# A retention and short-convolution step on one core: normalised y turned through DRAM and VectorE's block transposes, and both prompt-state products behind chunk 23

## The reference

```python
scores = jnp.einsum('bhld,bhmd->bhlm', q, k) * dmask
out = (jnp.einsum('bhlm,bhmv->bhlv', scores, v)
       + jnp.einsum('bhld,bhdv->bhlv', q, S) * q_decay[:, :, None])
S_new = S * s_decay[:, None, None] + jnp.einsum('bhmd,bhmv->bhdv', k * k_decay[:, :, None], v)
...
mu = jnp.mean(yf, axis=-1, keepdims=True)
var = jnp.mean(jnp.square(yf - mu), axis=-1, keepdims=True)
yn = ((yf - mu) * lax.rsqrt(var + GN_EPS)).astype(h.dtype)
yn = yn.transpose(0, 2, 1, 3).reshape(B, L, RET_V)
return (jax.nn.silu(g) * yn) @ w_out, S_new
```

## Time and profile before

| what | value |
|---|---|
| median of 3 runs | 1662.14 us (1662.13 to 1662.34) |
| the profiled execution | 1662.3 us |
| its span, first to last instruction | 1660.7 us |
| granted TensorE clock, mean | 0.997 |
| PE busy | 1641.7 us (99%) |
| DVE busy | 1048.8 us (63%) |
| ACT busy | 594.8 us (36%) |
| POOL busy | 163.3 us (10%) |
| data moved by DMA | 338.47 MB, 204 GB/s |

### The profile page before, as it was taken

One profiled execution on the slowest core, in us unless ns is written; L12 is line 12 of the kernel. 1 busy time (PEld: TensorE's weight loads), 2 busy tenths in 40 slices (PEclk: granted clock), 3 DMA queues, 4 the chain that ended last, 5 costly groups with the idle time before them and its releaser, 6 DMA issues.

```text
span 1660.7 us, 30156 instructions
## 1 busy us (share of the span) xinstructions
PE 1641.7 (99%) x10864; PEld 1582.0 (95%) x10864; DVE 1048.8 (63%) x1671; ACT 594.8 (36%) x814; POOL 163.3 (10%) x241
## 2 busy tenths in 40 slices
PE   9999999999999999999999999999999999999996
PEld 9999989989999999999998998999999999999995
DVE  6566556556656656656655655977766666666465
ACT  4333333333333333333233333543333334343333
POOL 1001101101100100100100110510000000000243
PEclk9999999999999999999999999999999999999998
DMA  8647947946855864884794793445744444444442
GB/s 324 215 143 259 321 139 256 316 139 224 318 192 171 310 229 156 279 294 142 264 323 135 256 325 116 156 136 182 257 153 146 152 144 144 147 151 143 146 146 101
DMA packets 125208, 338.47 MB, mean 204 GB/s; under 512 B 27248, under 2 KB 43248, under 8 KB 125120
## 3 DMA queue, kind: packets, MB, share of 16 engines
q1 hardware_dynamic: 104768, 263.10, 47.4%
q0 software_dynamic: 20352, 74.08, 12.5%
HBM read 280.08 MB, written 46.28 MB: 197 GB/s over the span
## 4 chain that ended last, share of the span: by engine, by line
PE 97%; ACT 1%; DVE 1%; DMA 0%; issue 0%; POOL 0%; SPq 0%; ACTq 0%; DVEq 0%; POOLq 0%
PE proj L1313 25%; PE proj L1318 25%; PE proj L1314 25%; PE proj L1450 5%; PE proj L1458 4%; PE proj L1451 4%; PE qs L1409 2%; PE side L1297 1%; PE side L1299 1%; PE side L1298 1%; PE side L1341 1%; PE side L1304 1%; ACT residual L692 0%; PE proj L1476 0%; PE qs L1414 0%; PE side L1380 0%
## 5 line engine op out<-in xcount | busy, mean ns | idle before, releaser
L1313 PE MATMUL proj<-x_hi,w_hi 128*128 128x322 f32 (+2 forms) x2512 | 763.0, 314 | 0.0
L1314 PE MATMUL proj<-x_lo,w_hi 128*128 128x322 f32 (+2 forms) x2512 | 759.1, 312 | 0.0
L571 ACT CAST w_hi<-w_raw 128x1024 fp32r<-128x1024 f32 x416 | 436.1, 1049 | 588.3 <-PE proj L1314 386.9
L812 DVE TENSOR_TENSOR w_lo<-w_raw,w_hi 128x1024 fp32r<-128x1024 f32 x416 | 512.2, 1234 | 146.2 <-ACT w_hi L571 91.9
L1313 PEld LDWEIGHTS proj<-x_hi,w_hi 128*128 128x128 f32 x2512 | 473.8, 189 | 5.4 <-issue 4.4
L1314 PEld LDWEIGHTS proj<-x_lo,w_hi 128*128 128x128 f32 x2512 | 473.0, 188 | 0.4
L1318 PE MATMUL proj<-x_hi,w_lo 128*128 128x322 f32 (+2 forms) x2512 | 428.5, 313 | 0.3 <-DVE w_lo L812 0.3
L1318 PEld LDWEIGHTS proj<-x_hi,w_lo 128*128 128x128 f32 x2512 | 389.2, 189 | 0.5 <-DVE w_lo L812 0.5
L1450 PE MATMUL proj<-qk_or_z,w_hi 128*128 128x322 f32 x480 | 147.0, 316 | 0.6 <-DVE qk_or_z L1022 0.2
L1451 PE MATMUL proj<-qk_or_z,w_hi 128*128 128x322 f32 x480 | 144.0, 310 | 0.0
L844 DVE SCALAR_TENSOR_TENSOR state_update<-state_update,state_decay_of_head,side 128x512 f32<-128x512 f32 x128 | 94.0, 734 | 17.5 <-PE side L1341 14.5
(11 more groups left out here) (211 smaller groups left out, 1276.8 us busy)
## 6 DMA issues: line engine op xcount, KB each, us to landing
w_raw<-w_head SPq DMA_DIRECT2D x256, 512.0 KB, 4.4
w_raw<-w_conv SPq DMA_DIRECT2D x128, 512.0 KB, 3.5
state_update<-s_in POOLq DMA_DIRECT2D x64, 512.0 KB, 7.2
s_out<-state_update POOLq DMA_DIRECT2D x64, 512.0 KB, 5.6
te_for_q_or_prompt_state<-s_in SPq DMA_DIRECT2D x32, 512.0 KB, 7.6
w_raw<-w_cout SPq DMA_DIRECT2D x32, 512.0 KB, 3.5
v_scratch<-v_turned_or_y_norm SPq DMA_DIRECT2D x32, 176.0 KB, 5.4
v_rows<-v_scratch SPq DMA_DIRECT2D x8, 512.0 KB, 4.7
```

Source lines behind the costliest of these rows:

```text
L571: act.copy(w_hi[:, i % SPL, :], w_raw[:, i % RAW, :]).then_inc(w_h.sem, 1)
L812: TT(w_lo[:, i % SPL, :], w_raw[:, i % RAW, :], f(w_hi[:, i % SPL, :]), ALU.subtract).then_inc(w_l.sem, 1)
L1313: mm(bank[:, 0:n], wh[:, k, :], rhs_h(k), start=(first and k == 0), stop=False)
L1314: x = mm(bank[:, 0:n], wh[:, k, :], rhs_l(k), start=False, stop=False)
```

## The change

y's tiles are computed with full 128 rows, so that row r of tile t is token 128 t + r: 14 columns of zeros are put ahead of the first tile's scores (`A_AT`). TensorE makes the tiles in the order 0, 2, 1. VectorE takes all three statistics and the variance in side 19 and normalises in side 20, in that order too. SyncE stores each normalised tile (128 x 512, 256 KB) to a DRAM scratch ahead of its load of chunk 25, and ahead of its load of chunk 26 waits for the three stores and reads them back in four parts, so that 32 partitions hold one 32-token row of each of 12 blocks. In side 23 VectorE waits for the four reads and turns the 32 x 32 blocks in four instructions into PSUM, from where the gating reads as before. To fit the blocks, the columns of the gate's weights and the rows of the out weights are permuted on the host. The twelve transposes on TensorE are gone. Both groups of prompt-state products stand behind chunk 23, both of ScalarE's copies of them in side 24, ahead of them the fourth z part; and the stack copies of v that stood behind the loads of chunks 24 and 25 stand behind that of chunk 23.

```diff
-A_AT = [0, NP_ + NSAMP, NP_ + NSAMP + SC[1][1] + NSAMP]
+A_AT = [CUT, CUT + NP_, CUT + NP_ + SC[1][1]]
...
-VS_AT = {22: (8, 9, 10, 11), 23: (0, 1, 2), 24: (3, 4, 5), 25: (6, 7)}
+VS_AT = {22: (8, 9, 10, 11), 23: (0, 1, 2, 3, 4, 5, 6, 7)}
+Y_OUT, Y_BACK = 25, 26
...
+        y_b = vt_yn[:, :].rearrange("p (t n) -> p t n", t=YB)
+        y_dram = nc.dram_tensor("y_scratch", [YB, 32, DV], F32).ap()
+        yt_bank = [bank_r[2], bank_r[0], bank_r[1], bank_q]
...
+                    if i == Y_OUT:
+                        for n, t in enumerate((0, 2, 1)):
+                            sp.wait_ge(y_nm.sem, y_nm.at(h, n + 1))
+                            sp.dma_start(y_dram[4 * t:4 * t + 4, :, :].rearrange("a p n -> (a p) n"),
+                                         y_n[:, t, :]).then_inc(yd_out.sem, 16)
+                    if i == Y_BACK:
+                        sp.wait_ge(yd_out.sem, yd_out.at(h, yd_out.per))
+                        for a in range(4):
+                            sp.dma_start(y_b[32 * a:32 * a + 32, :, :],
+                                         y_dram[:, :, P * a:P * a + P].rearrange("t p e -> p t e")).then_inc(yd_in.sem, 16)
                     load_chunk(0, h, CPH, i, w_head[h, i])
...
-                        act.wait_ge(y_done.sem, y_done.at(h, 3))
+                        act.wait_ge(y_done.sem, y_done.at(h, 2))
                         act.copy(y_n[0:META, 2, :], bank_q[32:32 + META, :]).then_inc(yp_out.sem, 1)
                     if i == 24:
                         z_round(3)
-                    if i in (23, 24):
-
-                        d = i - 23
+                    for d in range(DKB) if i == 24 else ():
                         act.wait_ge(st_done.sem, st_done.at(h, d + 1))
...
+                    def turned(j):
+
+                        dve.transpose(yt_bank[j][:, 0:3 * P].rearrange("p (t e) -> p t e", e=32),
+                                      y_b[:, :, 32 * j:32 * j + 32]).then_inc(yt_done.sem, 1)
...
+                    if i == 23:
+                        dve.wait_ge(yd_in.sem, yd_in.at(h, yd_in.per))
+                        turned(0)
+                        turned(1)
+                        gated(0)
+                        turned(2)
+                        gated(1)
+                        z_rest(0)
+                        turned(3)
+                        gated(2)
+                        z_rest(1)
+                        z_rest(2)
+                    if i == 24:
+                        gated(3)
+                        z_rest(3)
...
-                    if i == 23:
-                        y_turn(3)
-                    if i in (22, 23):
-
-                        d = i - 22
+                    for d in range(DKB) if i == 23 else ():
                         if not d:
...
-                    if i == 22:
-                        y_turn(0, 1, 2)
...
-    w_v = w_in[:, 2 * qk:2 * qk + dv].reshape(D, HEADS, 4, DVB, 32).transpose(0, 1, 3, 2, 4).reshape(D, dv)
-    b = blocks(np.concatenate([w_in[:, 0:2 * qk], w_v, w_in[:, 2 * qk + dv:]], 1), 8)
+    w_vg = w_in[:, 2 * qk:].reshape(D, 2 * HEADS, 4, DVB, 32).transpose(0, 1, 3, 2, 4).reshape(D, 2 * dv)
+    b = blocks(np.concatenate([w_in[:, 0:2 * qk], w_vg], 1), 8)
...
-    wo = A(w_ret_out)[0].reshape(HEADS, DVB, P, KT // 2, 2 * P).transpose(0, 3, 2, 1, 4)
+    wo = A(w_ret_out)[0].reshape(HEADS, 4, DVB, 32, KT // 2, 2 * P).transpose(0, 4, 1, 3, 2, 5)
```

More of the change, by code:

```diff
@@ L54 @@
 A_LEN = A_AT[2] + SW
-Y_ROWS = [QRY[0][1], QRY[1][1], SW]
+YB = 3 * P // 32
 Y_TAIL = QRY[2][0] + 2 * META
@@ L244, in hybrid_step @@
         v_dram = nc.dram_tensor("v_scratch", [TB, 32, DV], F32).ap()
+        y_dram = nc.dram_tensor("y_scratch", [YB, 32, DV], F32).ap()
+        yd_out, yd_in = count("y_rows_out", 3 * 16), count("y_blocks_in", 4 * 16)
         tab_in = count("tab_in")
@@ L987, in side @@
                         dve.tensor_copy(sd_h[:, :], sdec[:, bass.ds(h, 1)]).then_inc(sd_set.sem, 1)
[L988 to L991, removed]
+                    if i == 19:
+                        for n, t in enumerate((0, 2, 1)):
+                            dve.wait_ge(y_done.sem, y_done.at(h, n + 1))
                             if t == 2:
@@ L996, in side @@
                                 dve.wait_ge(yp_add.sem, yp_add.at(h))
-                            dve.bn_stats(stat[0:rows, t, :], y_bank[t][0:rows, :]).then_inc(y_st.sem, 1)
-                            dve.wait_ge(y_st.sem, y_st.at(h, t + 1))
+                            dve.bn_stats(stat[:, t, :], y_bank[t][:, :]).then_inc(y_st.sem, 1)
+                            dve.wait_ge(y_st.sem, y_st.at(h, n + 1))
                             dve.sem_inc(passed.sem, 1)
-                            dve.bn_aggr(mv[0:rows, t, :], stat[0:rows, t, :]).then_inc(y_ag.sem, 1)
@@ L1001, in side @@
-                    if i == 20:
+                            dve.bn_aggr(mv[:, t, :], stat[:, t, :]).then_inc(y_ag.sem, 1)
                         dve.wait_ge(y_ag.sem, y_ag.at(h, 3))
                         dve.tensor_scalar(gvar[:, :], mv[:, :, 1], GN_EPS, None, add).then_inc(y_ve.sem, 1)
-                    if i == 21:
+                    if i == 20:
                         dve.wait_ge(y_rs.sem, y_rs.at(h))
[L1006 to L1022, removed]
+                        for t in (0, 2, 1):
+                            dve.tensor_scalar(y_n[:, t, :], y_bank[t][:, :], mv[:, t, 0:1], rstd[:, t:t + 1],
+                                              ALU.subtract, ALU.mult).then_inc(y_nm.sem, 1)
@@ new lines, in turned, with gated @@
+                    def turned(j):
+                        dve.transpose(yt_bank[j][:, 0:3 * P].rearrange("p (t e) -> p t e", e=32),
+                                      y_b[:, :, 32 * j:32 * j + 32]).then_inc(yt_done.sem, 1)
+                    def gated(j):
+                        dve.wait_ge(yt_done.sem, yt_done.at(h, j + 1))
+                        dve.wait_ge(p_act.sem, p_act.at(h, 1 + j))
+                        if j >= 2:
+                            dve.wait_ge(z_l.sem, z_l.at(h, j - 1))
+                        c0, c1 = CUT, CUT + Y_TAIL
+                        TT(tmp[:, j % 2, 0:Y_TAIL], yt_bank[j][:, c0:c1], gate[:, j, 0:Y_TAIL], ALU.mult)
+                        groups = yt_bank[j][:, c1:c1 + 96].rearrange("p (c i) -> p c i", i=32)[:, :, META:]
+                        rest = lambda ap: ap.rearrange("p (c i) -> p c i", i=META)
+                        TT(rest(tmp[:, j % 2, Y_TAIL:N]), groups, rest(gate[:, j, Y_TAIL:N]), ALU.mult).then_inc(z_f.sem, 1)
@@ new lines, in z_rest @@
+                    def z_rest(j):
+                        dve.wait_ge(z_h.sem, z_h.at(h, j + 1))
+                        TT(z_lo[:, j, :], tmp[:, j % 2, 0:N], f(z_hi[:, j, :]), ALU.subtract).then_inc(z_l.sem, 1)
+                    if i == 23:
[10 more added lines that the diff above has]
+                        z_rest(2)
@@ L1299, in three @@
                 return mm(out, a_lo_, b_hi_, start=False, stop=stop)
-            def turn(out, src):
-                n = src.shape[0]
-                return pe.transpose(out, src if src.dtype == F32 else src.bitcast(F32), ident[0:n, 0:n])
             def proj(base, r, per, i, bank, n, rhs_h, rhs_l, first, last, by_block=None):
@@ L1349, in head @@
             def head(h, first, last=False):
[L1350 to L1360, removed]
                 def side(i):
@@ L1418, in side @@
                         pe.wait_ge(a_l.sem, a_l.at(h, 3))
[L1419 to L1423, removed]
+                        at, kr = A_AT[2], KEY[2][1]
+                        for t in (0, 2, 1):
+                            if t == 2:
+                                x = three(bank_q[:, :], a_hi[0:kr, at:at + SW], a_lo[0:kr, at:at + SW], v_hi[0:kr, 2, :],
+                                          v_lo[0:kr, 2, :], False, True)
+                            for m in range(t + 1) if t < 2 else ():
+                                own = A_AT[m] + P * t - CUT - SC[m][0]
+                                x = three(bank_r[t][:, :], a_hi[:, own:own + P], a_lo[:, own:own + P],
                                           v_hi[:, m, :], v_lo[:, m, :], m == 0, m == t)
                             x.then_inc(y_done.sem, 1)
[L1426 to L1429, removed]
                     for back, t in due(KV_AT, i, first, last):
                         kv_multiply(h, t, back)
-                    if i == 22:
-                        y_turn(0, 1, 2)
                 def out(i):
```

## The result

The changed kernel takes 1685.7 us in the median (1683.4 to 1688.7, 4 runs); the kernel before, beside it, 1662.2. The ratio is 1.0141 (95% interval 1.0129 to 1.0153). Forecast were 1653.4 us and a range of 1649 to 1660, so the time moved 23 us the wrong way, and lies above the late case (1671) too.

What follows compares the result with a forecast made beforehand. TensorE was taken to bound the kernel. Per head, -1.28 (transposes) -0.31 (old wait) +0.5 (new wait) = -1.09 us; eight heads -8.7, so 1662.1 - 8.7 = 1653.4 us, range 1649 to 1660.

Steps and rivals of the forecast that it cites:

- the late case: Rival 2: the trip through DRAM takes v's prices, TensorE waits 2.7 us a head, 1671 us; chance 0.11.
- TensorE's part: In each head twelve transposes go, 1.28 us; y products and moved prompt-state products cost the same as before.
- the old wait: Before, the out product's weight load on TensorE waited for VectorE's z low part: 0.31 us a head, forecast to go.
- The price of the trip: y's stores and reads through DRAM on SyncE's queue: from the last store issued at 357.7 to landing at 366.5.
- The end of normalising: VectorE's third normalisation of y ends at 357.65, with GpSimd's power taking 0.88 us beside VectorE's low part.
- The stores: SyncE's three stores of normalised y tiles: the last issued at 357.7, landed 3.6 us later.
- The reads: SyncE's four reads of 192 KB: 1.6 us to the fourth issue, then 3.6 us to landing.
- My upper end: Bound on the trip from v's own trip under full DMA load, 4.7 us taken twice: reads landed at 368.7.
- S: Time at which the reads have landed and VectorE's first block transpose starts; forecast 366.5.
- From landing to z the chain: Block transposes, gating and z parts on VectorE and ScalarE: z part 3's low part ends at S + 7.6.
- The price of a wait: TensorE's new wait near chunk 24: near 0.5 us a head, with the clock taken as unchanged.
- Rival 2: The data is late: S = 368.7, wait 2.7 us a head against 1.59 saved, 1671 us; chance 0.11.

Runs made afterwards that it cites:

- the same idea in a better order: Changed kernel with chunk 20 ahead of statistics, reads ahead of chunk 25's load, chunk 24's cast before z high parts, fourth gate between second and third: 1652.5 us.

## Why the prediction was wrong, step by step

**TensorE's part was right.** Twelve transposes 1.18 us a head (1.28 forecast), the old wait 0.31, the moved state products nothing (the wait is all that their run gained). The wider y tile cost nothing that could be told: its products start 0.23 us apart, as before.

**The price of the trip was wrong, by 3.1 us a head.** In its steps, as means over the heads, from TensorE's arrival:

- The end of normalising: -14.4, forecast 357.65 - 372.83 = -15.2. 0.8 us late, all of it the power, which I took at the 0.88 of the earlier trace rows and called hidden beside VectorE. There the power had started ahead of VectorE's low part; here it starts just behind it, and takes 1.0 us more.
- The stores: 4.0 us to the reads' issue, forecast 3.65. Right to 0.4. The head's table, which the prediction named beside the stores and did not price, has a share by the trace: in head 7, which loads none, it was 2.9. In head 6 it was 6.0, and there GpSimd issued the table 1.3 us later than in the other heads, so that its packets lie among those of the stores. In every run with the trip head 7 is the quickest and head 6 slower than heads 1 to 5; none tests the cause.
- The reads: 7.1 us, forecast 1.6 + 3.6. 1.9 us late. I took the quiet row for a chunk alone, and noted that four reads and a chunk share the engines, but gave that no price. The run with nothing beside the reads gives it 1.2 us; the other 0.7 is the reads' own.

The sum is 3.1 us. My upper end had S at 368.7, or -4.1; the mean is beyond it, though I had called it a bound. It was no bound, for I had laid two trips of v's stores end to end, without the power and without a read's own price. The Trainium skill's price (DMA: Bandwidth & Descriptors, "Anatomy of one DMA"; fitted there on GpSimd's DMAs, per DMA) of 2.0 us and bytes over 436 GB/s would have made the trip shorter still, and doesn't fit here. By it the last read is estimated at 2.45 us, behind 1.6 us of issuing by the rows; the reads alone took 5.9 us from the first issue.

**From landing to z the chain was right to 0.4.** The low part of z part 3 ends at S + 7.2 in the heads (7.6 forecast), and the cast of chunk 24 at S + 5.2.

**The price of a wait was wrong.** I took none of the clock as changed, because a wait would be of a microsecond at most. The waits came to 3.2 us a head (25.2 over 8), and six heads of eight had products at half clock behind them, for 8 us in all. Rival 2, the late data, had the right mechanism and side, with chance 0.11, but without this term: it put 1671 where 1685.7 came.

**Where the wait stands.** The prediction looked for it on z part 3 alone; its chain has the cast at S + 5.6 (6.0 less the gate's 0.43), ahead of the arrival for as long as S is early. With S at -3.3 the cast ends at +2.0, and this is the mean first wait, which stands in no step of the prediction; z part 3 follows with 1.2 more. The sum of both is still set by z part 3.

Together, in the profiled execution: from the 8.7 us gain forecast to the loss of 21.1 (spans 1681.8 and 1660.7) there are 30 us. Waits are 21 of them (3.2 us a head where 0.5 were forecast: the landing 3.1 later, the chain behind it 0.4 quicker), the slower products 8 and the transposes 1. The median is 2 us above this execution, and no trace shows where those go.

**The Trainium skill's rule against the change** (VectorE: DVE Perf Modes, "Rules for kernel authors": a 128x128 transpose belongs on TensorE where PSUM will do) is right for the kernel as changed and wrong for the same idea in a better order: 1652.5 us against 1662.6. The fair rival of that order is the kernel before with its state products moved, at 1659.9; the trip in its good order is 7 us better than that.

## What to carry to other kernels

Work may be taken off a bound engine by a trip through memory, but then the trip is a race, and it has to be won with a margin: price each leg by a row under the load that it will meet, its own and its neighbours', and add the leg before it (here a reciprocal root on GpSimd). A wait on TensorE of one to three microseconds is to be priced above its length, since the clock behind it may fall: here it did in six heads of eight, at a third of the waits' own price. When data comes late, look first at what in-order queues put ahead of it: three reorderings without a new instruction took this kernel from 1686 to 1652 us.

## What of the hardware was not expected

- GpSimd's power on 128 x 3 elements takes 0.88 us when it starts before VectorE's 1.23 us subtraction or beside no work, and 1.86 us in the mean of 8 when it starts 0.09 us after it. That VectorE holds it up is shown by the run that moves the subtraction away; by what means is not.
- Reads in runs of 512 bytes with weight loads beside them go with full DMA engines at mostly 130 to 300 GB/s, and a 512 KB load beside them lands after 7.6 us, where one in the quiet stretch took 3.6. In the earlier trace rows v's stores have such runs too, and I had read their slowness as GpSimd's load alone.
- Twenty useless products in front of a wait made the kernel 9 us faster than the wait by itself.
